# A hybrid recurrent block on one core: input norm moved tile by tile into the first projection, and four staging places for the tail's inputs

## What is computed

```
u = rms_norm(h) * norm_g                         # mean of squares over 1024 channels
q,f,i,g,u_s,z_s,gate_hg,gate_s5 = split(u @ w_in)  # 8 heads x (q,f,i,g) of 128, then u_s 512, z_s 512, gates 2 x 1024
o = hgrn2(q, f, i)                               # chunkwise gated recurrence, 8 heads
y_hg = (rms_norm(o) * silu(g)) @ w_o_hg
ys = gelu(s5(u_s));  a,b = split(ys @ w_glu + b_glu);  ys = a * sigmoid(b) * silu(z_s)
h += (sigmoid(gate_hg) * y_hg + sigmoid(gate_s5) * (ys @ w_o_s5)) @ w_out
h += (p @ w_ple) * sigmoid(rms_norm(h) @ w_ple_gate)
return rms_norm(h)
```

## Time and profile before

| | |
|---|---|
| time, median of 3 runs | 2375.37 us (2375.15 to 2377.81) |
| the profiled execution | 2378.16 us, span of its instructions 2376.6 us |
| granted PE clock, mean | 0.979 of full |
| PE busy | 2272.8 us, 96% of the span |
| DVE, ACT, POOL busy | 1199.0, 919.9, 146.8 us |

### The profile page before, as it was taken

How to read it: one execution, slowest core, us unless ns; L and a number is a source line. 1 busy time by engine, 2 the same in 40 slices (tenths; PEclk the granted TensorE clock), 3 DMA queues, 4 the chain that set the end, 5 groups by cost and what they waited for, 6 DMA issues and landing times. The chain is left out here.

```text
span 2376.6 us, 30201 instructions
## 1 busy us (share of the span) xinstructions
PE 2272.8 (96%) x10800; PEld 1836.9 (77%) x10800; DVE 1199.0 (50%) x2230; ACT 919.9 (39%) x1360; POOL 146.8 (6%) x254
## 2 busy tenths in 40 slices
PE   6899999999999997999999999969999999999997
PEld 2688888888888886888777777758887777778775
DVE  5443444343444434111656566546566566665655
ACT  6343444443444434111233333333443354354343
POOL 0000000000000000110111111110001000100100
PEclk8899999999999999999999999989999999999998
DMA  4110101010100100322222222265336435634622
GB/s 160 36 36 23 45 9 44 9 49 18 35 26 26 41 18 14 86 65 85 78 78 87 87 77 80 77 202 167 118 114 212 153 99 177 212 107 135 219 90 79
DMA packets 89267, 206.37 MB, mean 87 GB/s; under 512 B 20832, under 2 KB 30048, under 8 KB 89184
## 3 DMA queue, kind: packets, MB, share of 16 engines
q1 hardware_dynamic: 68432, 139.68, 18.7%
q0 software_dynamic: 20752, 65.57, 8.3%
HBM read 157.87 MB, written 46.14 MB: 86 GB/s over the span
## 5 line engine op out<-in xcount | busy, mean ns | idle before, releaser
L95 PE MATMUL s_ps<-u_hi,s_w_hi 128*128 128x512 f32 x768 | 305.4, 398 | 8.7 <-DVE s_w_lo L875 8.7
L96 PE MATMUL s_ps<-u_lo,s_w_hi 128*128 128x512 f32 x768 | 300.0, 391 | 0.0
L97 PE MATMUL s_ps<-u_hi,s_w_lo 128*128 128x512 f32 x768 | 299.5, 390 | 0.0
L95 PE MATMUL t_ps<-t_oa_hi,t_w_hi 128*128 128x512 f32 x512 | 205.1, 401 | 13.8 <-DVE t_oa_lo L1555 9.9
L96 PE MATMUL t_ps<-t_oa_lo,t_w_hi 128*128 128x512 f32 x512 | 203.0, 396 | 2.5 <-issue 2.5
L97 PE MATMUL t_ps<-t_oa_hi,t_w_lo 128*128 128x512 f32 x512 | 202.7, 396 | 0.0
L1446 DVE TENSOR_TENSOR t_w_lo<-c_raw,t_w_hi 128x1024 fp32r<-128x1024 f32 x136 | 166.5, 1224 | 63.4 <-ACT t_w_hi L1352 63.4
L95 PEld LDWEIGHTS s_ps<-u_hi,s_w_hi 128*128 128x128 f32 x768 | 144.4, 188 | 52.6 <-issue 14.5
L97 PEld LDWEIGHTS s_ps<-u_hi,s_w_lo 128*128 128x128 f32 x768 | 144.5, 188 | 31.1
L96 PEld LDWEIGHTS s_ps<-u_lo,s_w_hi 128*128 128x128 f32 x768 | 144.6, 188 | 28.5
L1352 ACT ACTIVATE t_w_hi<-c_raw 128x1024 fp32r<-128x1024 f32 x136 | 142.4, 1047 | 41.7 <-PE t_ps L97 13.2
(11 more groups left out here) (280 smaller groups left out, 4786.6 us busy)
## 6 DMA issues: line engine op xcount, KB each, us to landing
c_raw<-w_in_in SPq DMA_DIRECT2D x56, 512.0 KB, 3.7
gates_scratch<-s_stage POOLq DMA_DIRECT2D x64, 256.0 KB, 2.7
t_ein<-gates_scratch SPq DMA_DIRECT2D x64, 256.0 KB, 4.4
c_raw<-w_o_hg_in SPq DMA_DIRECT2D x32, 512.0 KB, 5.0
c_raw<-w_out_in SPq DMA_DIRECT2D x32, 512.0 KB, 3.5
c_raw<-w_ple_gate_in SPq DMA_DIRECT2D x32, 512.0 KB, 3.5
c_raw<-w_glu_in SPq DMA_DIRECT2D x16, 512.0 KB, 4.2
t_xa<-o_gated_scratch POOLq DMA_DIRECT2D x32, 256.0 KB, 4.3
```

The costliest lines, as they stand in the source:

```text
L95: pe.matmul(out, w_hi, u_hi, start=first, stop=False)
L96: pe.matmul(out, w_hi, u_lo, start=False, stop=False)
L97: return pe.matmul(out, w_lo, u_hi, start=False, stop=last)
```

## The change

The part `phase_norm_in` is gone as a part of its own, and with it the barrier behind it. A new `phase_head` normalises a tile and at once projects it by the four U blocks (u_s), whose outputs it stores to `us_scratch` from the SP queue; then the same block runs the heads as before. So the four U blocks leave `phase_s5`, which now begins with the Z blocks (20 blocks, not 24). In `phase_head`:

- x stays whole in SBUF (`xs`, 4 tiles), is normalised in place, and `u_lo` is written over it. `sq` has four places.
- The sum of squares is made by PE for tile 0 (8 matmuls by ones); for tiles 1 to 3 POOL adds the eight squares (7 adds each, L260) and PE needs one matmul by ones a tile.
- The U weights 0 and 1 are split on ACT and DVE, 2 and 3 on ACT and POOL (L251), within tile 0.
- The table for Ln and Exp is loaded at the start.

```diff
+            def normed_blocks(t):
+                for half in range(2):
+                    pair = (2 * half, 2 * half + 1)
+                    if t == 0:
+                        pe.wait_ge((w_lo_done, w_lo_b_done)[half], 2)
+                    else:
+                        pe.wait_ge(u_staged, (t - 1) * S5KT + pair[1] + 1)
+                    for k in range(KT):
+                        if half == 0:
+                            pe.wait_ge(lo_done, t * KT + k + 1)
+                        elif k == 3 and t + 1 < NT:
+                            pe.wait_ge(added, (t + 1) * (KT - 1))
+                            pe.matmul((pk, pv)[(t + 1) % 2][:], c["ones"][:].bitcast(F32), sumsq[:, (t + 1) % 2],
+                                      start=True, stop=True).then_inc(xms_done, 1)
+                        for b in pair:
+                            ins = split_matmuls(pe, (pf, pg, pi, pq)[b][:], w_hi[:, b, k], w_lo[:, b, k],
+                                                u_hi[:, k, tile_of(t)], u_lo[:, k, tile_of(t)], k == 0, k == KT - 1)
+                            if k == KT - 1:
+                                ins.then_inc(u_filled, 1)
...
+            for t in range(1, NT):
+                for k in range(KT):
+                    round_u(t, k)
+                    if t + 1 < NT:
+                        square(t + 1, k)
+                    if k == 2:
+                        drain(t - 1, 2)
+                        drain(t - 1, 3)
+                for kind in range(2):
+                    drain(t, kind)
+                    if t == NT - 1:
+                        round_weights(0, kind)
+                if t + 1 < NT:
+                    one_over_rms(t + 1)
+            for kind in range(2, 4):
+                drain(NT - 1, kind)
                 round_weights(0, kind)
+            for sem in u_stored:
+                act.wait_ge(sem, NT * 16)
             heads(act, head)
...
+            for i in range(2):
+                pool.wait_ge(w_hi_b_done, i + 1)
+                pool.tensor_tensor(w_lo[:, 2 + i], raw_b[:, i], w_hi[:, 2 + i].bitcast(F32), ALU.subtract).then_inc(w_lo_b_done, 1)
+            for t in range(1, NT):
+                for k in range(1, KT):
+                    pool.wait_ge(sq_done, t * KT + k + 1)
...
+                    pool.tensor_tensor(sumsq[:, t % 2], before, sq[:, k % 4], ALU.add).then_inc(added, 1)
...
-    NB, U_BLOCKS, Z_BLOCKS = 24, S5KT, 2 * S5KT
+    NB, Z_BLOCKS = 20, S5KT
```

In the tail `xa` has four places (XS = 4), and POOL's wait for a load is for the split of the input four places back:

```diff
-    BANKS = 6
+    BANKS, XS = 6, 4
-        xa = m.sb("xa", [P, 2, TT])
+        xa = m.sb("xa", [P, XS, TT])
...
-                        load_xa(t * len(XBODY) + (len(XPRO) + n), n % 2, what, k, t if what == "p" else t + 1)
+                        base = len(XPRO) if isinstance(t, int) and t == 0 else t * len(XBODY) + len(XPRO)
+                        if n >= XS:
+                            splits = base + (n - XS + 1)
+                        elif first:
+                            splits = len(XPRO) - XS + n + 1
+                        else:
+                            splits = base - len(XBODY) + (LAST_USER[n] + 1)
+                        load_xa(splits, n % XS, what, k, t if what == "p" else t + 1)
             for n, (what, k) in enumerate(XPRO):
                 if what == "o":
-                    load_xa(n, n % 2, what, k, 0)
+                    load_xa(n - XS + 1, n % XS, what, k, 0)
```

More of the change, by code:

```diff
@@ L113, in prefetched, with phase_head @@
         sp.sem_inc(raw_in[half], 16)
-def phase_norm_in(nc, c, a, u_hi, u_lo):
+def phase_head(nc, c, a, xs, u_hi, u_lo):
     FIRST = 4
[L119 to L229, removed]
-                    if n >= 4:
-                        dve.wait_ge(lo_done, n - 3)
-                    dve.scalar_tensor_tensor(u[:, n % 4], xs[:, t % 3, k], c["norm_g"][:, k:k + 1], rstd[:, t % 2],
-                                             ALU.mult, ALU.mult).then_inc(u_done, 1)
-                    if n >= 2:
-                        split_lo(n - 2)
-                if t == 0:
-                    dve.wait_ge(lbe_done, 1)
-                    dve.tensor_tensor(lbs[:], lb2[:, 0], lb2[:, 1], ALU.add).then_inc(lb_done, 1)
-                    dve.wait_ge(lb_done, 4)
-                    dve.reciprocal(lbs[:], lbs[:]).then_inc(lb_done, 1)
-                    dve.wait_ge(lb_done, 5)
-                    dve.tensor_tensor(c["lb"][:], lb2[:, 0], lbs[:], ALU.mult).then_inc(lb_done, 1)
-                    dve.wait_ge(lb_done, 6)
-                    dve.tensor_scalar(c["omlb"][:], c["lb"][:], -1.0, 1.0, ALU.mult, ALU.add).then_inc(lb_done, 1)
-                    dve.tensor_scalar(c["nomlb"][:], c["lb"][:], 1.0, None, ALU.subtract).then_inc(lb_done, 1)
-            split_lo(NT * KT - 2)
-            split_lo(NT * KT - 1)
@@ new lines, in drain @@
+            def drain(t, b):
+                act.wait_ge(u_filled, t * S5KT + b + 1)
+                if t >= 1:
+                    act.wait_ge(u_stored[b], t * 16)
+                act.activation(stage[:, b].rearrange("p (j n) -> p j n", j=SC),
+                               (pf, pg, pi, pq)[b][:].rearrange("p (n j) -> p j n", j=SC), ACT.Copy).then_inc(u_staged, 1)
+            act.preload_act_table_set("natural_log_exp_and_others")
+            for k in range(KT):
+                square(0, k)
@@ new lines, in _ @@
+            for k in range(4, KT):
+                square(1, k)
+            drain(0, 0)
+            drain(0, 1)
+            act.wait_ge(lb_done, 3)
+            act.activation(lb2[:], lb2[:], ACT.Exp).then_inc(lbe_done, 1)
+            one_over_rms(1)
+            for t in range(1, NT):
+                for k in range(KT):
+                    round_u(t, k)
[10 more added lines that the diff above has]
+                    one_over_rms(t + 1)
@@ L1161, in loads_after @@
             return t * (UBODY // 2 * 16) + n if body else n
-        def x_buffer(body, what, k, half):
-            return (xn if not body and what == "y" and k >= 2 else xa)[:, half]
         def y_source(k, t):
@@ L1550, in split_x @@
                 hi, lo = (x[:, k] for x in dict(y=acts_y, o=acts_a, p=acts_p)[what])
-                src, hi = x_buffer(body, what, k, half), hi.bitcast(F32)
+                src, hi = xa[:, half], hi.bitcast(F32)
                 if what == "y":
```

212 lines of the change are left out of this document (170 added, 42 removed).

## The result

The changed kernel takes 2324.97 us (median of 4 runs, 2323.66 to 2326.18) against 2376.59 (2375.15 to 2385.66) of the kernel before in the same session: a ratio of 0.9774, 95% interval 0.9752 to 0.9795. It is 51.6 us faster. The forecast was 2302, range 2291 to 2318, so the direction was right and a third of the gain was missing. The profiled execution is 2326.18, span 2324.6; the sum of the prediction, made against the profiled execution before, said 2305.3.

The account below looks back on a forecast made before the run. PE's work plus its holes was taken as the bound (busy 2272.8 of 2376.6 us). Head 43.4 and tail 29.5 won make 72.9, taking the median 2375.4 to 2302.5, forecast as 2302; range of 8 in 10, 2291 to 2318.

Parts of the forecast that it names:

- Start at 20.0: Head: PE can start the first projection at about 20.0 us instead of 70.36, with the first rstd taken at 15.0.
- Projected tiles: Head's U blocks: 87.05 of matmuls, 1.5 cold start, 3.0 sums by ones and 4.0 charged slowness, ending at 115.5.
- shared slowness in tiles 0 to 2: Head: 4 us charged, between 0 and 12, for this and for POOL's close timing in tile 0.
- first rival: Head: POOL and DVE take turns by whole instructions, costing 12 to 14 us, not 4: 2311; chance 0.30.
- cold start, 1.5: Head: PE's first projections cost 1.5 us more, as it stood idle since the sums by ones.
- phase_s5 loses no cover: phase_s5 without the U blocks: parameters, weight splits and Z's first drain are still ready in time; cost nothing.
- Joints os5 to ohg: Tail: with four places for o inputs instead of two, the joints' loss of 20.2 becomes 1.2, 19.0 won.
- second rival: Tail: loads are bound by their transfer, not by the places; only 5 of 29.5 won, 2327; chance 0.08.
- Prologue: Tail's start, glu to os5: load of h still stands beside os5's weights; 2.8 of 9.8 kept, 7.0 won.
- ohg to out: Tail joint: stores start earlier and h and y2 come about 3 us earlier; 3.5 of 6.4 won.
- The third: Head and tail: adds at the lower bound, no stall, tail joints close fully; 4 + 5 more, 2293; chance 0.13.
- The fourth: Head: POOL's adds pace it, slower than before; needs 6.7 us an add, at 8 about 2403; chance 0.02.

Follow-up runs that it names:

- pe_warm: Changed kernel with idle PE time in the head filled by sums of a constant tile, 2 before the eight sums by ones and 6 behind: 2325.09 us.
- head_dve: Changed kernel with the head's 21 running sums of squares and two second weight splits on DVE instead of POOL, no work left out: 2315.38 us.
- unroll: Changed kernel with the tail's loop over tiles 1 and 2 written out on all engines, same instructions otherwise: 2318.72 us.
- old_unroll: Kernel before the change with only the tail's loop over input tiles written out: 2381.76 us beside 2379.42 of the kernel before.
- h_late: Changed kernel with the tail prologue's 2 MB load of h issued behind the last two o inputs instead of ahead of them: 2327.54 us.
- h_pieces: Changed kernel with the 2 MB load of h in eight 256 KB pieces, between other loads or behind each block's store: 2312.76 us.
- all4: Changed kernel with head sums and splits on DVE, h load in pieces, tail loop written out and PE kept busy in the head: 2296.53 us.

## Why the prediction was wrong

**Bound and size of the stalls: right, but for one cause.** PE's work plus its holes accounts for every stage, and what the first projection's start is worth followed from it. I put all the tail's stalls down to inputs, though; the largest hole of the prologue before was a wait for a weight split, 3.90.

**Start at 20.0: 1.5 short.** The first projection starts at 21.50. The step that failed is "I take the first rstd at 15.0": Exp ends at 16.75, later than the 16.10 before. The eight sums by ones take 9.44 at the start of the program, and the weight loads of PE in between stand 0.85 apart first and 0.43 later:

```profile
7.70 0.34 PEld L292 LDWEIGHTS hg_pk<-n_sq,c_ones 128*128 128x128 f32 x1 [0.52 <-issue]
8.55 0.34 PEld L292 LDWEIGHTS hg_pk<-n_sq,c_ones 128*128 128x128 f32 x1 [0.52 <-issue]
...
12.57 0.19 PEld L292 LDWEIGHTS hg_pk<-n_sq,c_ones 128*128 128x128 f32 x1 [0.24 <-issue]
13.00 0.19 PEld L292 LDWEIGHTS hg_pk<-n_sq,c_ones 128*128 128x128 f32 x1 [0.24 <-issue]
```

I moved a table load forward as if it were on the path. In the trace of before the sums end at 14.61, 0.12 ahead of the load's end, so little was to be won; in after they end at 15.30, with PE at half rate until about 10.8, not 8.4. `pe_warm` shows it: kept busy, PE is done with them by 13.6 and the first projection starts at 19.73.

**Projected tiles, 95.55 forecast, 102.48 measured.** Of this the matmuls are 87.05 as forecast, and the three sums 2.7 (22.67 less 21.76 each) instead of 3.0. Then:
- "this and shared slowness in tiles 0 to 2, I charge 4": measured 9.9, the difference between after's 102.48 and `head_dve`'s 92.59. This is the first rival, which I gave 0.30. It forecast 12 to 14. By the Trainium skill, "SBUF — State Buffer", "Who interferes with whom", the port pair shared by DVE and GpSimd is an exclusive lock. The trace agrees: every DVE instruction of 128x512 that is lengthened ends 0.54 to 0.56 behind the POOL instruction beside it, as if let in only when that was through, and takes 2.86 and 2.88 beside splits of 2.4 and 2.8, 1.78 beside an add. This step failed: the choice of 4 between 0 and 12 on the ground that no row showed POOL reading beside DVE. The absence of a row spoke for neither side.
- "cold start, 1.5": 2.8, what is left in `head_dve` of 92.59 - 87.05 - 2.7. The granted clock there is 0.50 (1.2 GHz) from 21.3 to 24 and 0.61 from 24 to 28, where the start at 70.36 before, after a longer pause of PE, cost 1.56; why it costs more here stays open. In after it lay under the first term (`pe_warm`), so 9.9 and 2.8 are the parts in this order of removal; taken out first, the cold start is worth nothing.
- POOL's prices were too low as well: a sum takes 1.29 to 1.76 (upper bound set: 1.16), a split 2.4 and 2.8 (2.3). Whether that gap counted was not separated.

**phase_s5 loses no cover: right within 0.9.** From the gated layer's first matmul to the first gate it is 0.9 more than before, with that kernel's U blocks and cold start taken out. Of this 0.7 lie ahead of the Z blocks, 0.2 of them in the wait for the first Z weights (8.92 where it was 8.74), and 0.2 in the Z blocks.

**Joints os5 to ohg, 19.0 forecast, 14.8 measured.** Joints 1 and 3 won 6.9 and 7.5 of the 7.1 each, by the mechanism as told; `t_xa` lands in 3.5 to 6.8 there. The second rival (transfers are the bound) is refuted at these two joints; its sign, `t_xa` loads of more than 10.9, does stand beside the loads of `h` (13.3 and 13.7 in the prologue, 14.5 at ohg to out). Joint 2 won 0.3 of 4.8. The step that failed is to treat the three alike: the trace of before has 2.47 of "issue" at exactly that joint, 2009.09, and I had booked it as a late input. `unroll` and `old_unroll` point to two causes in one hole. The profile doesn't say what "issue" is made of; that it goes when the loop is written out ties it to the loop's branch. The Trainium skill, "Runtime: NRT & Kernel Launch", "Instruction fetch mechanics", says that a taken branch to code outside the loaded pages stalls until it is fetched. The trace agrees as far as it goes: the 16 KB packet of instructions moves in PE's hole and is absent in `unroll`. It takes 0.9 us of the 3.42; what the rest is made of stays open.

**Prologue, 7.0 forecast, 2.1 measured.** The step that failed is "I keep 2.8 of 9.8": it keeps 6.7. The four places did their work, the inputs are not waited for. But the weights beside the 2 MB load were as late as the inputs before the change (1596.39 and 1596.16), and they stay late: PE waits 4.7 for weight splits there before and 4.6 after. I named this load as standing beside os5's weights, and worked out no price for it. `h_late` and `h_pieces` show that it holds what SP issues, on another queue, whoever comes at that time.

**ohg to out, 3.5 forecast, 0.1 measured.** The step that failed is to count the earlier start of the load of `h` as a gain alone: it now starts 4 us earlier relative to PE and meets the `w_out` weights, which take 10.9 at the first pass and 11.8 at the second (2.0 won at one, 1.9 lost at the other). `h_pieces` takes away both losses.

**Rivals 3 and 4.** The third (2293) did not come true; with four more edits `all4` comes to 2296.5. The fourth did not: POOL's adds were far from 6.7.

## What to carry to other kernels

Work that is moved to an idle engine is free only if the two engines don't hold each other up: here a sum given to POOL cost DVE more than making it. When an input stops being late, look in the trace for what landed just beside it, and look for the largest transfer in flight on any queue; cut it, since moving it here only picked another victim. A hole in front of a loop's first unit can have two causes one behind the other; then each cure alone shows little, and only both together do. And run a kernel that is unchanged in a stage before you read a small gain there: here an untouched tail moved by 6 us.
